# A hybrid delta-net, SSD and expert-choice block on one core: the late modulation taken up block by block between the first convolutions, two wide decay differences, and the token choice in two halves

## The reference

```python
mod_lat = split(silu(c) @ ada_w + ada_b, 6)            # six rows of 1024; four of them are needed late
h       = modulate(rms_norm(x, g0), mod_lat[0], mod_lat[1])
proj    = h @ w_in                                     # conv channels | z | gates
u       = silu(depthwise_conv3x3(proj[conv channels])) # q, k, v, x, B, C
# gated delta rule (4 heads) and SSD (8 heads), both directions, chunked:
decay   = where(tri, exp(G_i - G_j), 0)
x2      = x + mod_lat[2] * rms_norm(merge(...) @ w_out, g1)
h2      = modulate(rms_norm(x2, g2), mod_lat[3], mod_lat[4])
aff     = softmax(h2 @ router_w)                       # 1024 tokens x 16 experts
gate, idx = top_k(aff.T, 128)                          # each expert takes its 128 best tokens
y[idx] += (silu(h2[idx] @ wg) * (h2[idx] @ wu)) @ wd * gate
out     = x2 + mod_lat[5] * rms_norm(y, g3)
```

## Time and profile before

| what | value |
|---|---|
| median of three runs | 1633.59 us |
| the profiled execution: its own time | 1629.44 us |
| its span, first to last instruction | 1627.6 us |
| mean granted TensorE clock | 0.916 |
| PE busy | 1331.3 us (82%) |
| DVE busy | 864.7 us (53%) |
| ACT / POOL busy | 439.4 us (27%) / 214.6 us (13%) |
| chain that ended last, by engine | PE 53%, DVE 22%, DMA 9%, ACT 8%, issue 4% |

### The profile page before, as it was taken

The page is one execution under the profiler, slowest core; times in us unless marked ns, Lnnn a source line. Parts: engine busy times, 40 slices in busy tenths (PEclk is TensorE's granted clock), DMA queues, the critical chain, the costliest instruction groups (busy, mean ns, idle before and its releaser), DMA issues.

```text
span 1627.6 us, 13873 instructions
## 1 busy us (share of the span) xinstructions
PE 1331.3 (82%) x5055; PEld 774.9 (48%) x5055; DVE 864.7 (53%) x1243; ACT 439.4 (27%) x935; POOL 214.6 (13%) x190
## 2 busy tenths in 40 slices
PE   6898899999992999678788878989207999999990
PEld 1354444444452555468787774444203444444440
DVE  1257556679778466468889964555591110010115
ACT  1525524521101122244444433343101011110102
POOL 0003100210000000144444510000000110111100
PEclk9899899999995999799999998999557999999995
DMA  8204122224683000244545453332605999999936
GB/s 309 74 26 137 42 58 75 66 58 154 209 256 103 13 26 0 61 142 127 151 133 162 145 194 142 130 131 102 234 37 192 341 335 343 333 331 331 333 80 219
DMA packets 185689, 257.80 MB, mean 158 GB/s; under 512 B 48861, under 2 KB 107990, under 8 KB 185622
## 3 DMA queue, kind: packets, MB, share of 16 engines
q1 hardware_dynamic: 169078, 225.30, 41.4%
q0 software_dynamic: 7040, 25.17, 5.5%
q10 hardware_dynamic: 9504, 6.45, 1.3%
HBM read 212.38 MB, written 44.50 MB: 158 GB/s over the span
## 4 chain that ended last, share of the span: by engine, by line
PE 53%; DVE 22%; DMA 9%; ACT 8%; issue 4%; SPq 2%; POOL 0%; POOLq 0%; DVEq 0%; ACTq 0%
PE ps L1537 18%; PE ps L997 14%; PE ps L1016 6%; PE ps L352 5%; DVE arena L541 5%; DMA arena<-ada_w 3%; DMA arena<-zt_dram 2%; DVE arena L1891 2%; PE ps L962 2%; PE ps L1495 2%; DMA arena<-g_dram 2%; DVE arena L1908 1%; DVE arena L1232 1%; DVE arena L1950 1%; DVE arena L1948 1%
## 5 line engine op out<-in xcount | busy, mean ns | idle before, releaser
L1537 PE MATMUL ps<-arena 128*128 128x512 f32 (+1 forms) x1120 | 444.9, 557 | 0.0
L1537 PEld LDWEIGHTS ps<-arena 128*128 128x128 f32 x1120 | 214.2, 193 | 217.9 <-issue 212.7
L1891 DVE SCALAR_TENSOR_TENSOR arena<-arena,taps 128x1024 f32<-128x1024 f32 x160 | 227.0, 1419 | 5.7
L997 PE MATMUL ps<-arena 128*128 128x512 f32 x512 | 227.3, 597 | 1.4 <-ACT arena L1114 1.4
L352 PE MATMUL ps<-arena 128*128 128x128 f32 x1088 | 154.6, 304 | 67.5 <-ACT arena L507 48.3
L352 PEld LDWEIGHTS ps<-arena 128*128 128x128 f32 x1088 | 146.8, 216 | 78.9 <-ACT arena L507 55.1
L997 PEld LDWEIGHTS ps<-arena 128*128 128x128 f32 x512 | 96.7, 192 | 117.2 <-issue 115.2
L541 DVE SCALAR_TENSOR_TENSOR arena<-arena,G,neg_mask 128x128 f32<-128x128 f32 x208 | 121.3, 648 | 27.6 <-DMA arena<-g_dram 27.5
L1245 DVE TENSOR_TENSOR arena<-arena,ps 128x512 f32<-128x512 f32 x16 | 11.0, 687 | 225.6 <-PE ps L997 225.6
L962 PE MATMUL ps<-arena 128*128 128x512 f32 x256 | 116.2, 609 | 4.6 <-ACT arena L1062 4.6
L1016 PE MATMUL ps<-arena 128*128 128x512 f32 x256 | 112.6, 593 | 1.2 <-DVE arena L1252 1.2
(11 more groups left out here) (268 smaller groups left out, 1576.6 us busy)
## 6 DMA issues: line engine op xcount, KB each, us to landing
arena<-exp_w_gate SPq DMA_DIRECT2D x16, 2048.0 KB, 11.2
arena<-exp_w_up SPq DMA_DIRECT2D x16, 2048.0 KB, 9.0
arena<-exp_w_down SPq DMA_DIRECT2D x16, 2048.0 KB, 11.0
arena<-ada_w SPq DMA_DIRECT2D x16, 1024.0 KB, 6.2
arena<-w_in SPq DMA_DIRECT2D x28, 512.0 KB, 3.9
arena<-ada_w SPq DMA_DIRECT2D x4, 2048.0 KB, 10.5
arena<-x SPq DMA_DIRECT2D x16, 512.0 KB, 9.0
arena<-g_dram SPq DMA_DIRECT2D x16, 512.0 KB, 3.8
```

What stands on the lines that cost most here:

```text
L997: last = mm(ps[gu_bank[s] + j][:], xsT[s][:, k, :], ew[s][j][:, k, :], start=(k == 0), stop=(k == KD - 1))
L1537: last = mm(ps[3 * (m % 2) + gi][:, 0:w], wring[(m + 1) % NW][:, k, :], hT[:, k, o:o + w], start=(k == 0), stop=(k == KD - 1))
L1891: ins = v.scalar_tensor_tensor(accg, cin_l[ci % 2][:, j // 3:j // 3 + GR, j % 3:j % 3 + GW], tp[:, j:j + 1], accg, ALU.mult, ALU.add)
```

## The change

1. The 16 blocks `late(b)` move on DVE to behind the first twelve convolutions, 1, 1, 1, 1, 2, 2, 1, 1, 1, 1, 1, 3 of them. The `late` jobs move to the ends of `jobs[6]`, `[8]`, `[12]` and `[14]`. SP's loads of the blocks move into its turns m = 3 to 14, ahead of that turn's stores. The sums get eight slots in turn; the two buffers lie elsewhere; the second clearing of the padded inputs and ACT's wait for it go. POOL's masking of the inverse's inputs now waits for the job `late` 2 as well.
2. `diff` is two TENSOR_TENSORs over all its heads (512 or 1024 elements) with a link between them, in place of one instruction to a head.
3. The token choice works on 32 rows of 512 (two halves of the tokens of 16 experts), takes 128 of each half, and then the larger of the one half's i-th and the other half's (127 - i)-th.

```diff
+        N_LATE = [1, 1, 1, 1, 2, 2, 1, 1, 1, 1, 1, 3]
+        for i, m in enumerate((6, 8, 12, 14)):
+            jobs[m] += [("late", i, 0)]
...
             def diff(out, t, d, g0, n):
-                for h in range(n):
-                    last = v.scalar_tensor_tensor(out[:, h, :], out[:, h, :], G[:, t, d, g0 + h:g0 + h + 1],
-                                                  neg_mask[:, d, :], ALU.subtract, ALU.min)
-                return last
+                link(v.tensor_tensor(out, out, bc(G[:, t, d, g0:g0 + n], P), ALU.subtract))
+                return v.tensor_tensor(out, out, bh(neg_mask[:, d, :], n), ALU.min)
...
-            v.tensor_copy(topf, topi).then_inc(sem("route"), 1)
+            v.tensor_copy(topf, topi)
+            v.tensor_copy(topfr, topi[:, ::-1])
+            v.tensor_copy(topvr, topv[:, ::-1]).then_inc(sem("route"), 1)
             dve.wait_ge(sem("affps"), 2)
...
+            link(v.tensor_copy(flat(two), ps[0][:, 0:4 * E2]))
+            v.tensor_tensor(pick[:, 0], va, vb, ALU.is_ge)
+            link(v.scalar_tensor_tensor(pick[:, 1], ia, float(TH), ib, ALU.subtract, ALU.subtract))
+            link(v.tensor_tensor(pick[:, 1], pick[:, 1], pick[:, 0], ALU.mult))
+            link(v.scalar_tensor_tensor(pick[:, 1], pick[:, 1], float(TH), ib, ALU.add, ALU.add))
...
             for m in range(NM):
                 s = (m + 1) % NW
                 if m + 1 >= NW:
                     sp_.wait_ge(sem("w_used"), m + 1 - NW + 1)
                 col = tiles[m][0]
                 sp_.dma_start(wring[s], w_k[:, :, col:col + P]).then_inc(sem(f"w_in{s}"), 16)
+                if m >= NW - 1:
+                    upto = min(sum(N_LATE[:m - NW + 2]) + 2, NLB)
+                    for b in range(n_late, upto):
+                        late_load(b)
+                    n_late = upto
 
                 mj = m - 4
                 for kind, i, part in (jobs[mj] if mj >= 0 else []):
...
             pool.wait_ge(sem("bin"), 16 * 11)
+            pool.wait_ge(sem("aux"), AUX[("late", 2, 0)] + 1)
...
+            b = 0
+            for m in range(M_Z0):
+                conv(m)
+                for _ in range(N_LATE[m]):
+                    late(b)
+                    b += 1
...
-            for b in range(NLB):
-                late(b)
-
-            dve.wait_ge(sem("aux"), AUX[("late", 0, 0)] + 1)
-            for i in range(2):
-                v.memset(cin_l[i], 0.0).then_inc(sem("pad"), 1)
-                v.memset(cin_c[i], 0.0).then_inc(sem("pad"), 1)
```

More of the change, by code:

```diff
@@ L168, in hybrid_block @@
         x1_f = arena[:, STG0:STG0 + 1024]
[L169 removed]
+        xc1_f = kb_f
+        tmp_f = kb1_f[:, 0:720]
         CTX0, CTX1 = slice(0, BL), slice(BL, 2 * BL)
@@ L800, in hybrid_block @@
         x2 = take(NL * D).rearrange("p (t n) -> p t n", t=NL)
-        affT = take(T)[0:E_N, :]
+        E2, TH = 2 * E_N, T // 2
+        affT = take(TH)[0:E2, :]
         row5 = take(D)
@@ L804, in hybrid_block @@
         sqj = take(D)
-        tk = take(3 * P)
-        topv, topf = tk[0:E_N, 0:CAP], tk[0:E_N, CAP:2 * CAP]
-        topi = take(P).bitcast(U32)[0:E_N, 0:CAP]
+        tk = take(4 * P).rearrange("p (r n) -> p r n", r=4)
+        topv, topf, topvr, topfr = (tk[0:E2, r, :] for r in range(4))
+        topi = take(P).bitcast(U32)[0:E2, 0:CAP]
+        two = take(4 * E2).rearrange("p (r n) -> p r n", r=4)
+        pick = take(2 * E_N).rearrange("p (r n) -> p r n", r=2)
         idxT = take(E_N).bitcast(U32)
@@ L1106, in act_tail @@
             act.wait_ge(sem("affps"), 1)
-            for h in range(2):
-                a(affT[:, h * 512:(h + 1) * 512], ps[2 + h][0:E_N, :], ACT.Copy).then_inc(sem("lexp"), 1)
+            a(affT, ps[2][0:E2, :], ACT.Copy).then_inc(sem("lexp"), 1)
             def xs_copy(e, h):
@@ L1603, in _ @@
                         for q in range(8):
-                            last = mm(bank[:, q:q + 1], lsum[4 * i + q // 2][:, (q % 2) * P:(q % 2 + 1) * P], ones[:, 0:1],
+                            last = mm(bank[:, q:q + 1], lsum[(4 * i + q // 2) % 8][:, (q % 2) * P:(q % 2 + 1) * P], ones[:, 0:1],
                                       start=True, stop=True)
@@ L1663, in take_tile @@
                         act.wait_ge(sem("pad"), 4)
-                    if tiles[m][1] == "v" and tiles[m][2] == 0:
-                        act.wait_ge(sem("pad"), 8)
                     if ci >= 2:
@@ L1895, in conv @@
                 ins.then_inc(sem("conv"), 1)
-            for m in range(M_Z0):
-                conv(m)
             def late(b):
-                blk = lring[b % 2]
+                blk, out = lring[b % 2], lsum[b % 8]
                 dve.wait_ge(sem(f"ada_in{b % 2 + 1}"), 16 * (b // 2 + 2))
-                if b == 4:
-                    dve.wait_ge(sem("xy_out"), 128)
-                link(v.tensor_scalar(lsum[b], blk[:, 0, :], silu_c[:, 0, 0:1], None, ALU.mult))
+                if b >= 8:
+                    dve.wait_ge(sem("aux"), AUX[("late", b // 4 - 2, 0)] + 1)
+                if b == 6:
+                    dve.wait_ge(sem("y_zero"), 16 * 2 * NL)
+                link(v.tensor_scalar(out, blk[:, 0, :], silu_c[:, 0, 0:1], None, ALU.mult))
                 for k in range(1, KD):
-                    ins = v.scalar_tensor_tensor(lsum[b], blk[:, k, :], silu_c[:, k, 0:1], lsum[b], ALU.mult, ALU.add)
+                    ins = v.scalar_tensor_tensor(out, blk[:, k, :], silu_c[:, k, 0:1], out, ALU.mult, ALU.add)
                     if k < KD - 1:
```

46 lines of the change are left out of this document (18 added, 28 removed).

## The result

The changed kernel takes 1637.88 us at the median against 1630.41 for the kernel before (20 runs each): a ratio of 1.0041, with a 95% interval of 1.0031 to 1.0050, so 7.5 us slower. The profiled execution took 1637.84 us, its span 1635.7 and its mean granted clock 0.913. The forecast was 7.5 us faster.

| place | before | changed | lead or lag | change in the stage |
|---|---|---|---|---|
| tile 14 starts | 373.81 | 485.69 | +111.9 | predicted +89.5 |
| tile 21 starts (end of Part A) | 530.95 | 605.20 | +74.3 | A: +74.3, predicted +52.3 |
| last 8-head difference of the scan | 959.34 | 994.33 | +35.0 | B: -39.3, predicted -35 |
| first expert on PE (line 997, now 1003) | 1233.59 | 1241.60 | +8.0 | C, and 2 of the tail: -27.0, predicted -25 |

The account below looks back on a forecast made before the run. PE is held up by late blocks on DVE in the projection loop, the scan by a chain through DVE, token choice by DVE alone. Profiled 1629.44 + 50 - 33 - 25 = 1621.4, as median 1626 us; range 1595 to 1652.

Parts of the forecast that it names:

- Part A: Projection loop: late modulation moved between convolutions; SP's stores wait for late blocks, so it loses +50 us.
- the price of the chain: Convolutions 7 to 11: convolution, late block, SP, landing and ACT no longer overlap; 29.2 us a tile in place of 19.8.
- Landing 1.6 and SP 5.0: Two links per tile: the last small store lands in 1.6 us; SP's load and two kk stores take 5.0.
- The upper bound of +65: Worst case for the moved late modulation: each landing 3.8 us in place of 1.6, six times.
- Part B: Scan: two wide differences beside POOL in place of eight narrow operations; 13.65 us a step, before 15.93; -33 us.
- The 4.0 us of a difference: Scan: two wide operations take two turns with POOL's products, 4.0 us in place of 6.62.
- five steps in six of the fast kind: Scan at 0.92 granted clock: most steps at full clock, 13.5 us, the others 14.5; mean 13.65.
- the rival: Scan: wide operations hold up POOL's products, POOL becomes late, steps 14.65 us or more; 1640 us; chance 0.18.
- the waits behind all products: Scan rival: each wide operation waits for all POOL's products; difference 7.9 us, +20 in place of -33; 1679 us; chance 0.06.
- the kept port: Scan rival: DVE isn't interrupted between its two wide operations; difference 3.0 us, -50; 1609 us; chance 0.10.
- C has its full gain: Answers a token-choice rival: instructions cost by count, not length, so halves gain about 0; 1651 us; chance 0.03.
- Part C: Token choice on two halves: 47 DVE instructions shorter by 0.533 us each, all on the path; -25 us.

Follow-up runs that it names:

- The runs on SP's order: Changed kernel with each turn's late loads behind its stores: 1563.03 us; or still ahead, but waiting for one convolution earlier in turns 8 to 13: 1570.17 us.
- The run with 128 KB loads: Changed kernel, each late load bringing one of a block's eight row groups, which DVE uses eight times; other late weights left out: 1620.47 us.
- Part B alone: Kernel before with only the two wide operations of `diff`: 1589.23 us, ratio 0.9739.
- the four-operation run beside POOL: Kernel before with only the wide `diff`, each difference split into two pairs of operations over half its heads: 1625.71 us, ratio 0.9982.
- the one with lagged loads: Changed kernel, late loads still ahead of the stores, but in turns 8 to 13 waiting for the late block of one convolution earlier: 1570.17 us.

## Why the prediction was wrong

**Part A's mechanism held, its size did not.** Every link named was found: late block, SP's load and stores, landing, ACT's copy, silu, the tile's copy; so was the third job ahead of tile 13. The runs on SP's order show it as the cause (75 us by five lines). The step that failed is the price of the chain, 29.2 us a tile and tile 14 at 463.3; it was 31 and 485.7. With A at its measured cost the forecast of a gain turns into the loss. These terms were mis-sized:
- *Landing 1.6 and SP 5.0.* They were taken from a kernel in which no 1 MB load is under way beside these stores. I had counted the moved load's issue (0.4) but not its transfer. With it the stores land in 3.9, those of ktok in 7.4 in place of 4.1, and the two kk take 6.0 on SP. The run with 128 KB loads gives the size: 14.0 of the 22.4 us at tile 14, and 17.4 in the time. The upper bound of +65 had a landing of 3.8, close to this, but by a misreading: the 3.8 belongs to the load of the inverse, and the slowest of the stores took 2.7.
- *The rest, 8.4.* With small loads convolution 7 was still 3.3 late and convolution 11 6 late; these 6 us are not taken apart. From there to the inverse's first part it was 2 more: the prediction let the inverse's loads land in 1.7 us, but the last of them, of 512 KB, took 4.1 there (3.8 in the kernel before), and DVE stood idle 7.5 us for it. The three late blocks behind convolution 11 were done by then, so they are not what held the inverse in these two runs; once the order on SP is mended they are.

From tile 14 to 21 it was 119.5 us, predicted 119.9.

**Part B was undersized.** The 4.0 us of a difference came out as 3.95, but the steps around it were misread. The step of 16.61 us was called one at half clock; the granted clock over it was 0.90 (columns as in the earlier trace rows):
```profile
770.29:786.90 16.61, 13.46 (x98) 12.78 (x98) 14.37 (x26) 6.80 (x20) 6.93 (x7) 0.90 0.47 142
```
And a clock of 0.92 does not make five steps in six of the fast kind: in that same stretch of the kernel before, twelve of the 15 steps took 15.7 to 16.6 us and only two 13.6. That the new steps would be mostly fast had thus no row behind it. They are all fast: 1.00 over the scan, 13.31 a step on average and not 13.65, where the mean before was 15.91. That is 39.0 in 15 steps, and -39.3 in the stage where the prediction had -35. Part B alone gave 42.5 in time (37 to 48 by its interval), its steps at 13.4 and a clock of 0.99. POOL's product did stretch to 2.25, as the rival said, but PE never waited for POOL in these 15 steps: its idle time there is 22.1 us, for ACT and DVE, where it was 48.7 before. That rival is out. So are the others: 3.95 us for the difference rules out the waits behind all products (7.9) and the kept port (3.0); C has its full gain; and the distance of the convolutions shows that SP's order did bite. What limits a step now is in part another thing: the loads from g_dram are 30% of the chain that ended last in the 8-head steps, and were 7%.

**Part C** was right: -26.6 alone, -25 predicted.

**The sum.** 50 - 33 - 25 gave -8; measured by parts it is 73.6 - 42.5 - 26.6, or +4.5, and +7.5 together. Set like against like, by the stages, A missed by +22, B by -4.3 and C by -2. So the misses of B and C took back 6 us of A's. The time lies in the range of 1595 to 1652, and even in the forecast's own 1612 to 1643, but Part A lay outside the +45 to +60 from which that was made: that the sum came so near is partly luck. It lies on the side that had a chance of 0.28, though by none of the mechanisms named for that side: it was the forecast's own chain, longer. "I take +50, as each link has its row" overlooked that each row came from a kernel without the moved transfers.

The rule cited of the Trainium skill, page "VectorE: DVE Perf Modes", section "Rules for kernel authors" (keep the count of operations in a chain small), agrees with the four-operation run beside POOL: 6.00 us against 3.95 for the same elements.

## What to carry to other kernels

When work moves to another place, list its DMAs with it: each has a wait that holds the queue behind it, and bytes that slow the small transfers near it. Ahead of small stores on which another engine waits, a load that waits for the engine to be unblocked closes a ring, and the pitch becomes the sum of all links; one that waits for work of one round earlier closes none, wherever it stands. Place small PE jobs where the bank that they need is free without a store. Where DVE works beside POOL's products, count the operations and not only the elements.

## What was not expected

- The same slow landing costs in a closed chain and not in an open one: it was 3.9 us at the median in both the changed kernel and the one with lagged loads. In the first, smaller transfers, with the shorter landings and issues that come with them, gave 17 us; in the second the convolutions kept their distance of 18.97 all the same.
- SP's issue of the small stores is slower right behind a large load: 2.26 to 2.35 us for the first four on kb_dram of a turn, in place of 1.88 in most turns before (2.52 in one), and 1.89 again with 128 KB loads.
- The scan's granted clock rose from 0.92 to 1.00 when DVE's part became shorter; in its steps PE is busy 177.72 of 199 us (89%) where it was busy 192.60 of 239 (81%), and idles 22.1 us where it idled 48.7. With four operations in place of two the difference is shorter by 0.6 us only, and the clock stays at 0.92. That the shorter waits hold the clock up is my reading; no run held them apart.
